# Spare transpositions in the opening, and three orders changed: the third conv slot's halves, the output products, the last down bank

## The reference

```python
mod = silu(c) @ ada_w + ada_b                       # sh1, sc1, g1, sh2, sc2, g2
xn = rmsnorm(x, norm1_g) * (1.0 + sc1) + sh1
q, k, v, ca, cg = split(xn @ w_in)
y_attn = attention(q, k, v, rel_bias)               # 8 heads of 64, causal, with QK-norm
a = silu(group_norm(causal_dwconv(ca * sigmoid(cg), width 31)))
x = x + g1 * (concat(y_attn, a) @ w_out)
xn2 = rmsnorm(x, norm2_g) * (1.0 + sc2) + sh2
u, g = split(causal_dwconv(xn2 @ w_up, width 3))
x = x + g2 * ((silu(g) * u) @ w_down)               # 2816 hidden columns
```

## Time and profile before

| what | value |
|---|---|
| time, median of 3 runs | 341.64 us (340.95 to 342.36) |
| time of the profiled execution | 342.01 us |
| its span | 340.1 us |
| TensorE busy | 328.6 us, 97% of the span |
| VectorE, ScalarE, GpSimd busy | 259.9, 192.1, 78.8 us |
| mean granted TensorE clock | 0.994 |
| moved by DMA | 80.00 MB, mean 235 GB/s |

### The profile page before, as it was taken

One profiled execution on the slowest core, in us unless ns is written; L12 is line 12 of the kernel. 1 busy time (PEld: TensorE's weight loads), 2 busy tenths in 40 slices (PEclk: granted clock), 3 DMA queues, 4 the chain that ended last, 5 costly groups with the idle time before them and its releaser, 6 DMA issues.

```text
span 340.1 us, 5700 instructions
## 1 busy us (share of the span) xinstructions
PE 328.6 (97%) x2113; PEld 272.8 (80%) x2113; DVE 259.9 (76%) x523; ACT 192.1 (56%) x309; POOL 78.8 (23%) x121
## 2 busy tenths in 40 slices
PE   7779999999999999999999999999999999999995
PEld 6547988878665689998888888888888878888983
DVE  1564699998867557477997898989898686878766
ACT  4633745417457785549876656565656556565520
POOL 7392079657971500300000000000000001000000
PEclk9989999999999999999999999999999999999999
DMA  7999989999996952405455585767675456610003
GB/s 269 430 418 417 418 337 292 315 368 357 345 417 237 431 201 93 156 2 215 158 183 189 181 312 189 299 201 291 227 278 228 152 217 190 199 69 0 0 2 123
DMA packets 15291, 80.00 MB, mean 235 GB/s; under 512 B 1686, under 2 KB 3102, under 8 KB 8096
## 3 DMA queue, kind: packets, MB, share of 16 engines
q1 hardware_dynamic: 14864, 78.97, 62.0%
q0 software_dynamic: 256, 0.54, 0.8%
q10 hardware_dynamic: 144, 0.13, 0.1%
HBM read 78.57 MB, written 1.06 MB: 234 GB/s over the span
## 4 chain that ended last, share of the span: by engine, by line
PE 89%; DVE 3%; DMA 2%; POOL 2%; issue 1%; ACT 1%; SPq 0%; POOLq 0%; ACTq 0%
PE bank L1663 22%; PE bank L1217 13%; PE bank L1218 12%; PE bank L1219 12%; PE bank L1664 11%; PE bank L1240 3%; DMA raw<-in_stream 2%; PE bank L1541 2%; PE bank L1542 2%; PE bank L1543 2%; PE bank L1279 2%; PE bank L1484 1%; PE bank L1503 1%; PE bank L1492 1%; PE bank L1657 1%
## 5 line engine op out<-in xcount | busy, mean ns | idle before, releaser
L1663 PE MATMUL bank<-act_parts,w_hi 128*128 128x512 f32 x320 | 113.4, 398 | 0.0
L474 ACT ACTIVATE w_hi<-raw 128x2048 fp32r<-128x2048 f32 x41 | 78.5, 1915 | 22.1 <-DMA raw<-in_stream 17.0
L1664 PE MATMUL bank<-act_parts,w_lo 128*128 128x256 f32 x320 | 89.7, 280 | 0.0
L780 DVE TENSOR_TENSOR w_lo<-raw,w_hi 128x2048 fp32r<-128x2048 f32 x33 | 75.3, 2284 | 2.7 <-ACT w_hi L474 2.7
L1663 PEld LDWEIGHTS bank<-act_parts,w_hi 128*128 128x128 f32 x320 | 60.1, 188 | 15.0 <-DVE w_lo L780 0.2
L1664 PEld LDWEIGHTS bank<-act_parts,w_lo 128*128 128x128 f32 x320 | 60.4, 189 | 0.4
L408 POOL TENSOR_TENSOR w_lo<-raw,w_hi 128x512 fp32r<-128x512 f32 (+1 forms) x48 | 51.4, 1104 | 31.4 <-DMA raw<-in_stream 11.9
L1217 PE MATMUL bank<-act_parts,w_hi 128*128 128x256 f32 x144 | 42.7, 297 | 1.6 <-ACT act_parts L515 1.1
L906 DVE SCALAR_TENSOR_TENSOR bank<-glu,cols,bank 128x227 f32<-128x227 f32 (+28 forms) x116 | 44.1, 468 | 0.0
L1218 PE MATMUL bank<-act_parts,w_hi 128*128 128x256 f32 x144 | 41.0, 285 | 0.0
L1219 PE MATMUL bank<-act_parts,w_lo 128*128 128x256 f32 x144 | 41.0, 284 | 0.0
(11 more groups left out here) (214 smaller groups left out, 533.3 us busy)
## 6 DMA issues: line engine op xcount, KB each, us to landing
raw<-in_stream SPq DMA_DIRECT2D x55, 1024.0 KB, 5.9
raw<-in_stream SPq DMA_DIRECT2D x32, 512.0 KB, 6.8
xt<-in_x_t SPq DMA_DIRECT2D x2, 512.0 KB, 4.6
bias<-toeplitz_rows SPq DMA_DIRECT2D x1, 1024.0 KB, 12.1
xt<-in_x_t SPq DMA_DIRECT2D x1, 1024.0 KB, 6.8
out<-xmod SPq DMA_DIRECT2D x3, 256.0 KB, 2.0
gate<-gate_rows POOLq DMA_DIRECT2D x2, 256.0 KB, 6.7
gates_b<-in_ada_b_gates SPq DMA_DIRECT2D x1, 256.0 KB, 8.9
```

The costliest lines, as they stand in the source:

```text
L474: nc.scalar.activation(w_hi[:, m % PARTS, :], slot(*SPLIT[m]), ACT.Copy).then_inc(hi_done, 1)
L780: nc.vector.tensor_tensor(w_lo[:, m % PARTS, :], slot(*SPLIT[m]), w_hi[:, m % PARTS, :].bitcast(f32), ALU.subtract).then_inc(lo_done, 1)
L1663: nc.tensor.matmul(o[:, :], wh, act_parts[:, 2 * k:2 * k + 2, :], start=first, stop=False)
L1664: return nc.tensor.matmul(o[:, 0:SEQ], wl, act_hi[:, k, :], start=False, stop=last)
```

## The change

It has four parts. First, six spare transpositions come ahead of `ada_rows(2)` and eight behind `first_products(1, (0,))`. Second, ScalarE's two halves of the third conv slot stand ahead of and behind `xn_high(7)`. Third, two of the four tiles of `out_part(0, tiles_a)` come ahead of `pair_scores(3)`. Fourth, the end: VectorE adds gate times bank 3 into the residual after down slot 8; the last two down slots first do banks 0 to 2, and their share of bank 3's columns goes into two other banks (4 and 7, which the up slots used) in halves of 256 columns. VectorE does product and sum of each half; GpSimd has no part in it any more. No matmul of the down product is added except by halving: 12 of 512 columns become 24 of 256.

```diff
@@ scalar
-                if k >= KT - 2:
-                    first_pair_hi(k - KT + 2)
+                if k == KT - 1:
+                    first_pair_hi(0)
                 xn_high(k)
+            first_pair_hi(1)
@@ tensor, opening
             ada_columns(1)
+            keep_clock(6, 5)
             ada_rows(2)
             ada_columns(2)
             first_products(1, (0,))
+            keep_clock(8, 5)
             first_products(2, (0,))
@@ tensor, attention
             head_turn(5)
+            out_part(0, range(0, 2))
             pair_scores(3)
-            out_part(0, tiles_a)
+            out_part(0, range(2, 4))
             pair_values(2)
@@ tensor, the end (down(i) stays for i < LAST_DOWN - 1 = 9)
+            def last_downs():
+                one, two = LAST_DOWN - 1, LAST_DOWN
+                ready(SP_AT["down", one])
+                hidden_ready(one, 1)
+                for b in range(2 * ST - 1):
+                    for f in range(2):
+                        down_product(bank[b][:, :], one, f, b, 0, 512, False, False)
+                ready(SP_AT["down", two])
+                for b in range(2 * ST - 1):
+                    for f in range(2):
+                        hidden_ready(two, f)
+                        last = down_product(bank[b][:, :], two, f, b, 0, 512, False, f == 1)
+                    last.then_inc(down_done, 1)
+                for h in range(2):
+                    o = bank[LAST_BANK[h]][:, 0:256]
+                    for i in (one, two):
+                        for f in range(2):
+                            last = down_product(o, i, f, 2 * ST - 1, 256 * h, 256 * h + 256, i == one and f == 0, i == two and f == 1)
+                    last.then_inc(down_done, 1)
@@ vector, the end
+            dve.wait_ge(w_used, SP_AT["down", LAST_DOWN - 2] + 1)
+            nc.vector.tensor_tensor(tmp[:, 1, :], bank[done][:, :], gate[:, 0, half[1]], ALU.mult).then_inc(out_part, 1)
+            dve.wait_ge(out_part, 1)
+            nc.vector.tensor_tensor(xr[:, ST - 1, half[1]], xr[:, ST - 1, half[1]], tmp[:, 1, :], ALU.add).then_inc(out_base, 1)
...
-            dve.wait_ge(down_done, 2 * ST)
-            dve.wait_ge(out_ready, 2)
-            for a in (0, 256):
-                nc.vector.tensor_tensor(tmp[:, 1, a:a + 256], bank[2 * ST - 1][:, a:a + 256], gate[:, 0, 512 + a:768 + a],
+            for h, a in enumerate((512, 768)):
+                dve.wait_ge(down_done, done + h + 1)
+                dve.wait_ge(out_ready, 2)
+                nc.vector.tensor_tensor(tmp[:, 1, 256 * h:256 * h + 256], bank[LAST_BANK[h]][:, 0:256], gate[:, 0, a:a + 256],
                                         ALU.mult).then_inc(out_part, 1)
-            dve.wait_ge(out_part, 2 * ST + 1)
-            nc.vector.tensor_tensor(out_rows[:, 2 * ST - 1, 256:], xr[:, ST - 1, 768:], tmp[:, 1, 256:],
-                                    ALU.add).then_inc(out_ready, 1)
+                dve.wait_ge(out_part, done + h + 2)
+                nc.vector.tensor_tensor(out_rows[:, done, 256 * h:256 * h + 256], xr[:, ST - 1, a:a + 256],
+                                        tmp[:, 1, 256 * h:256 * h + 256], ALU.add).then_inc(out_ready, 1)
@@ gpsimd
-            pool.wait_ge(out_part, 2 * ST)
-            nc.gpsimd.tensor_tensor(out_rows[:, 2 * ST - 1, 0:256], xr[:, ST - 1, 512:768], tmp[:, 1, 0:256],
-                                    ALU.add).then_inc(out_left, 1)
```

More of the change, by code:

```diff
@@ L276, in hymba_layer @@
         WIDE = range(1, FT - 1)
+        LAST_DOWN, LAST_BANK = FT // 2 - 1, (4, 7)
         PAIRS = HEADS // 2
@@ L765, in _ @@
                     hid_high(t)
-            act.wait_ge(out_ready, 2 * ST)
+            act.wait_ge(out_ready, 2 * ST + 1)
             act.dma_start(out[ST - 1, :, 768:], out_rows[:, 2 * ST - 1, 256:]).then_inc(stored, 16)
@@ L1190, in _ @@
                     g2_products(t - 1)
+            half = [slice(h * 512, h * 512 + 512) for h in range(2)]
+            done = 2 * ST - 1
             dve.wait_ge(gate2_ready, 32)
             dve.wait_ge(x2_rows, 2 * ST)
-            for i in range(2 * ST - 1):
-                half = slice((i % 2) * 512, (i % 2) * 512 + 512)
+            dve.wait_ge(w_used, SP_AT["down", LAST_DOWN - 2] + 1)
+            nc.vector.tensor_tensor(tmp[:, 1, :], bank[done][:, :], gate[:, 0, half[1]], ALU.mult).then_inc(out_part, 1)
@@ L1196, in _ @@
+            dve.wait_ge(out_part, 1)
+            nc.vector.tensor_tensor(xr[:, ST - 1, half[1]], xr[:, ST - 1, half[1]], tmp[:, 1, :], ALU.add).then_inc(out_base, 1)
+            for i in range(done):
                 dve.wait_ge(down_done, i + 1)
-                if i == 2:
+                if i == 1:
+                    dve.wait_ge(out_base, 1)
+                elif i == 2:
                     dve.wait_ge(out_ready, 1)
-                nc.vector.tensor_tensor(tmp[:, i % 2, :], bank[i][:, :], gate[:, 0, half], ALU.mult).then_inc(out_part, 1)
@@ L1200, in _ @@
-                dve.wait_ge(out_part, i + 1)
-                nc.vector.tensor_tensor(out_rows[:, i, :], xr[:, i // 2, half], tmp[:, i % 2, :], ALU.add).then_inc(out_ready, 1)
-            dve.wait_ge(down_done, 2 * ST)
-            dve.wait_ge(out_ready, 2)
-            for a in (0, 256):
-                nc.vector.tensor_tensor(tmp[:, 1, a:a + 256], bank[2 * ST - 1][:, a:a + 256], gate[:, 0, 512 + a:768 + a],
+                nc.vector.tensor_tensor(tmp[:, i % 2, :], bank[i][:, :], gate[:, 0, half[i % 2]], ALU.mult).then_inc(out_part, 1)
@@ L1207, in _ @@
+                dve.wait_ge(out_part, i + 2)
+                nc.vector.tensor_tensor(out_rows[:, i, :], xr[:, i // 2, half[i % 2]], tmp[:, i % 2, :], ALU.add).then_inc(out_ready, 1)
+            for h, a in enumerate((512, 768)):
+                dve.wait_ge(down_done, done + h + 1)
+                dve.wait_ge(out_ready, 2)
+                nc.vector.tensor_tensor(tmp[:, 1, 256 * h:256 * h + 256], bank[LAST_BANK[h]][:, 0:256], gate[:, 0, a:a + 256],
                                         ALU.mult).then_inc(out_part, 1)
-            dve.wait_ge(out_part, 2 * ST + 1)
@@ L1716, in down @@
                 pe.wait_ge(hid_hi_ready, 2 * i + 2)
[L1718 to L1727, removed]
@@ L1728, in down, with down_product @@
-                if i < FT // 2 - 1:
-                    last.then_inc(w_used, 1)
+                for f in range(2):
+                    for b in range(2 * ST):
+                        last = down_product(bank[b][:, :], i, f, b, 0, 512, i == 0 and f == 0,
+                                            i == LAST_DOWN - 2 and f == 1 and b == 2 * ST - 1)
+                last.then_inc(w_used, 1)
+            def down_product(o, i, f, b, begin, end, first, closes):
+                t, n = b // 2, b % 2
+                place = (2 * i + f) % 4
+                h = (hid_hi[:, place, t * P:(t + 1) * P], hid_lo[:, place, t * P:(t + 1) * P])
+                return product(o, h, weights(SP_AT["down", i], f * D_MODEL + n * 512 + begin, end - begin), first, closes)
@@ new lines, in hidden_ready @@
+            def hidden_ready(i, f):
+                pe.wait_ge(hid_lo_ready, 2 * i + f + 1)
+                pe.wait_ge(hid_hi_ready, 2 * i + f + 1)
+            def last_downs():
[14 more added lines that the diff above has]
+                    for i in (one, two):
+                        for f in range(2):
+                            last = down_product(o, i, f, 2 * ST - 1, 256 * h, 256 * h + 256, i == one and f == 0, i == two and f == 1)
+                    last.then_inc(down_done, 1)
@@ L1733, in _ @@
             for kind, i in UP_DOWN[2:]:
-                (up if kind == "up" else down)(i)
+                if kind == "up":
+                    up(i)
+                elif i < LAST_DOWN - 1:
+                    down(i)
+            last_downs()
 def _layout(x, c, rel_bias, ada_w, ada_b, norm1_g, w_in, q_norm_g, k_norm_g, conv_dw_w, conv_dw_b, conv_norm_g,
```

5 lines of the change are left out of this document (2 added, 3 removed).

## The result

The changed kernel takes **339.48 us** (median of 12 executions, 338.63 to 340.62) against 342.25 us for the kernel before (12 executions, 340.95 to 344.74): ratio 0.9913, 95% interval 0.9892 to 0.9935, so 2.8 us less. The forecast was 339.4 us.

A forecast was written before the change was run, and what follows sets the result against it. TensorE, busy 328.6 of 340.1 us, was taken to bound the kernel, with its few waits and what follows its last matmul. 1.3 + 0.7 + 0.6 = 2.6 us off 342.01 gave 339.4 us, range 338.7 to 340.0.

The forecast's parts named there:

- Edit 1: Opening: spare transpositions keep TensorE at 2.4 GHz, saving 1.55 us of low clock for 0.3 delay; 1.3 us net.
- Rival (a): Opening: the clock falls all the same, or fell only in the profiled run; transpositions cost 0.3 us; 341.0 us, chance 0.17.
- Edit 2: Third conv slot: VectorE's low halves start 0.57 us late, ending in a later wait; cost nothing, at most 0.57 us.
- Rival (c): Conv pair 2, 41.97: TensorE waits 0.6 us for the late split and the clock falls there; 343.2 us, chance 0.05.
- The load at 85.31: TensorE's 0.17 us wait for a load stays about as is; if the load did not move, all 1.3 us end there.
- Rival (b): Clock holds, but about half the gain ends at a load (85.31) or late split (41.97); 340.1 us, chance 0.10.
- Edit 3: Attention, ahead of the scores at 118.84: two output tiles fill TensorE's 0.72 us wait; 0.7 us saved, bounds 0.5 to 0.74.
- Edit 4: End: VectorE work behind the last matmul falls from 1.60 to 0.9 us, smaller matmuls cost 0.1; 0.6 us saved.
- Rival (d): Attention tiles and end give a third of their sums, since another engines' chain ends last; 340.3 us, chance 0.08.

The follow-up runs named there:

- after_third: The changed kernel itself, nothing altered, run again beside the kernels with the bias transfer moved: 339.45 us, ratio 0.9927 to the kernel before.
- only_end: The kernel before with the new end alone (VectorE's output products, the stores, the last down slots): 342.02 us, ratio 0.9992.
- before_bias: The kernel before with the 1 MB attention bias transfer issued behind the load of `out` 0: 341.83 us, ratio 0.9998.
- no_spare: The changed kernel without the fourteen spare transpositions, its other three parts kept: 340.30 us, ratio 0.9934 to the kernel before.
- only_tiles: The kernel before with only two output tiles moved ahead of `pair_scores(3)`: 341.12 us, ratio 0.9968.
- only_open: The kernel before with the fourteen spare transpositions and the new places of the third conv slot's halves: 340.79 us, ratio 0.9958.

## Why the prediction was right, and where it was lucky

**Sum.** For two executions that start alike, before and after_third, the table gives A 1.29 us, B 0.02, C 0.14, D 0.74, E 0.69: 2.88 of the 2.90 us between 342.01 and 339.11. Forecast were 1.3, 0, 0, 0.7 and 0.6.

**Edit 1, 1.3 us.** As a size for an execution with one stretch it held: 1.29 us in A. The working held too: 0.3 us of delay (`first_products(2)` at 22.35 in after_third, where rows 3 have 22.08 from a like start; the waits fell to 0.50 and 0.43, where I had 0.45 and 0.3), and the low clock gone. As a term of the median it failed, in two ways that cancel. I took the one fall of the profile as what every execution has; the mean clocks fit 0 to 3, and where there is none the fourteen cost their 0.3 us: for late starts A is 34.95 (from 11.38) and 35.06 (from 11.53) with them, and 34.61 (from 11.30) and 34.75 (from 11.56) without. And I took it that TensorE arrives 1.3 us earlier to the end. By removal the fourteen are worth 0.6 us in the median, as far as 12 executions against 6 can tell. Rival (a) is out: no execution with the fourteen has a stretch at 0.50 in its mean clock. The clock page of the Trainium skill ("TensorE: Matmul & The Clock Gate", Part 1, on oscillation), read as at the time of the forecast, would have had no fall behind two waits of about 1 us. Before and only_end have it behind them and before_bias in the second of them, no_spare and only_tiles have none; the measurement decides, and it says "sometimes".

**Edit 2, nothing.** Right as a cost: no wait came at conv pair 2. The low halves started at 39.75, not at the 40.4 that I had, since `xn_high(7)` and the second half behind it moved 0.6 us forward with TensorE. Rival (c) needed one there and is out. But the step left unpriced what the old order would have cost an earlier TensorE. I had written that ScalarE's first half "would hold that one to the landing, which an earlier TensorE can't move", and put no number on it: 0.8 us in the median, 1.2 in the profile. That is the term that the sum lacked. Edits 1 and 2 are best taken as one; together they gave 1.48 us (only_open), 1.3 in the forecast.

**The load at 85.31.** The step "its issue follows TensorE's own work too, so this wait stays about as it is" held in two of three profiles of the changed kernel: the load of `out` 0 came 1.0 and 1.4 us earlier (86.7 and 86.3 against 87.7), and C is 53.09 and 53.08 against 53.22. In the first profile it failed: `out` 0 landed at 87.9, although TensorE came 0.7 us earlier. What the step lacked is that a landing differs by about a microsecond from execution to execution, against a TensorE whose wait there was 0.17, and that the copy `qk_rows` is queued behind the split that waits for it. Rival (b) is what the first profile shows, though at another instruction than the two it named: 0.82 us lost in C, time 340.62. The median, 339.48, is near the sum without such a loss, and the waits of 0.5 us of the other two profiles stood in the kernel before as well.

**Edit 3, 0.7 us.** 0.7 to 0.9. TensorE's wait was filled as worked out, and nobody waited for `att_lo_part(3)`.

**Edit 4, 0.6 us.** 0.5 to 0.7. From the first down matmul to the end of the last one it is 164.46 us before and 164.49 after, so the smaller matmuls cost 0.03 us and not 0.1, and 0.7 us less stands behind them, as worked out. Rival (d), a third of both terms, is out by D and E.

So for edits 3 and 4, and for two executions with a like start, 339.4 came true by its working. For the median it took luck too: a too simple clock term (one fall, always; 0.6 us by removal in place of 1.3) and a missing gain of edit 2 (0.8 in place of nothing) stood against each other, 1.4 together. What stays open: where the further low time of the kernel before lies, and whether it is several stretches or a longer one, since each profiled execution had at most one stretch; why SyncE took 1.70 us for one issue; and whether the late start itself prevents the fall or only goes with it, since five profiles stand behind that.

## What to carry to other kernels

A stall that one execution shows may be absent in the next, or cost several times as much; look at the mean clock of all executions before giving it a price, and ask of a cure what it costs where the stall isn't. A load that is waited for by a few tenths of a microsecond in one execution can take a gain of the compute engines in another, since its landing here differed by a microsecond: find these loads, and what is queued on the waiting engine behind its wait for them. A transfer that lands long before it is used can go behind one that is waited for, which here gave another 0.5 to 0.7 us.

## What the runs showed of the hardware that was not expected

- The mean granted clock of the kernel before was 0.983 to 1.000, with nothing changed in the program, in four clusters that fit 0 to 3 stretches of 3.4 us at half clock (67 executions: 15, 28, 16 and 8). The profiles show none or one.
- Waits of 0.91 and 1.09 us were followed by no fall (no_spare), 0.90 and 1.09 us at the same places by one (before).
- The same matmuls at 5.8 us (sixteen in the profile's count) took 3.72 to 6.04 us, so that `ada_rows(0)` started at 10.0 or at 11.3 to 11.8. Of 1.8 us of late start, 0.65 were left at `ada_rows(7)` (35.30 against 34.65), as waits behind took up the rest.
- The load of `out` 0 took 8.9 to 11.1 us from issue to landing in six profiles (the table of landings).
